# Embedding product and memory projection in five pieces at five places between the experts of a two-block kernel

## The chip, the cores and the metric

The kernel runs on one core of a Trainium2 chip. The time is that of one execution of the whole program on the device, in microseconds (us); a smaller one is better.

## The reference

Two transformer blocks follow each other on 256 tokens of width 1024, all in float32. The first has pooling and neighbourhood attention, an expert layer (16 experts, each takes its 32 best tokens), and an embedding that is mixed in behind it. The second has sparse, recurrent and memory attention and a feed-forward part. What the change touches, cut to its core:

```
# expert layer: each expert e takes its 32 tokens xe of h
a = xe @ w_gate[e]; b = xe @ w_up[e]          # 32x1024 @ 1024x2048
ye = (silu(a) * b) @ w_down[e]                # 32x2048 @ 2048x1024
x[tokens of e] += gate * ye                   # 16 experts

# embedding, first block: needs only p and w_ple_proj
e = rms_norm(p @ w_ple_proj, norm_ple_post)   # 256x256 @ 256x1024
x = x + sigmoid(rms_norm(x, norm_ple) @ w_ple_gate) * e

# memory keys and values, second block: need only mem and w_kv
kv = rmsnorm(mem, g_mem) @ w_mem_kv           # 256x1024 @ 1024x1024
k, v = kv[:, :512], kv[:, 512:]
```

The embedding product and the memory projection depend on nothing that the experts compute, so they may stand at any place between them.

## The kernel before, in words

**The ring.** Weights pass through a ring of six slots in SBUF of 2 MB each (`ring`, lines 205 and 206); three other buffers serve as slots 6, 7 and 8 for expert 0 only: `later`, `turned_T` and `gains`. Each slot has two semaphores, `full` (a load has landed) and `free` (it may be written again). `Ring.load` (line 161) waits for `free` of its slot and issues the load (line 169); `Ring.arrived` (line 176) is the other side. SyncE (SP) issues all weight loads, in one fixed order written out by hand; while it waits for one slot, no later load is issued, even where its slot lies free.

**An expert.** It has twelve loads of 2 MB: n = 0 to 3 for the gate, 4 to 7 for up, 8 to 11 for down. `around(rot)` gives the slots: load n goes into slot (n + rot) mod 6, so each slot serves twice. TensorE's `expert` (line 965) gathers the 32 tokens (32 matmuls) and the gate values (16 small ones), waits for `xe_sb`, which VectorE gives when it has scaled the gathered input (line 1514), multiplies slot by slot with 16 matmuls of 512 columns each, hands a slot back after its last matmul, transposes the hidden values (line 993), multiplies by the down weights, and adds the result to the tokens (8 matmuls, line 1011). ScalarE and VectorE evict in between (lines 621 to 630 and 1512 to 1527); VectorE adds to x (line 1526). The slot of the last load, n = 11, is handed back at the very end (line 1014).

**The order.** `PARTS = (1, 5, 5, 5)`: expert 0 is written out, and then come three loops over five experts, each a body of its own in the code of every engine. What lies between the loops is written out by hand on each engine:

- behind expert 5 (lines 1025 to 1052 of TensorE): four transposes of p (line 1029), the 16 transposes of the normed memory (`turn(1, mx, 0)`, line 839), the embedding product from slot 3 (16 matmuls of 512 columns), and the first half of the memory projection, the keys, from slot 4 (64 matmuls of 256 columns), evicted by ScalarE into `later` (line 656), whereupon slot 4 is handed back (line 1052);
- behind expert 10 (lines 1055 to 1061): the second half, the values, from slot 2 (32 matmuls of 512 columns), evicted at line 661.

ScalarE evicts the embedding product (line 647) and sums its squares (line 653). VectorE turns the memory into its transposed and scaled form (line 1397), waits for the squares (line 1539) and for the rows (line 1540), computes the inverse root (from line 1369) and scales the embedding (line 1543). The rows are four loads that ScalarE issues right behind expert 0 (lines 638 to 640) into `gains`, which is free only then; they are written to all 128 partitions.

**Slots at the two breaks.** The loop before the first break ends on slot 2; then come slot 3 (embedding, 1 MB), slot 4 (memory, 2 MB) and the loop that begins with slot 5. That loop ends on slot 4; then comes slot 2 (memory, 2 MB), and the last loop begins with slot 3. Slots 5, 0 and 1 are passed over there.

Of the kernel before, what the change touches and what calls it, by code (L numbers as in the profile page):

```python
# [46 lines left out]
PARTS = (1, 5, 5, 5)  # L47
# [77 lines left out]
FIRST_SLOTS = [0, 1, 2, 3, 6, 8, 4, 5, 7, 0, 1, 2]  # L125

# [68 lines left out]
def two_blocks(nc, a, out):  # L195
    ctx = ExitStack()
    with ctx:
# [215 lines left out]
        def _(sp):  # L413
# [3 lines left out]
            def whole(s, name, i):  # L417

                n = a[name].shape[2]
                return slot[s][:, 0:n], packed[name][bass.ds(i * P, P), :]  # L420
# [20 lines left out]
            def experts(part, rot):  # L441
                with sp.Fori(0, PARTS[part]) as i:
                    r.enter(i, {s: (2, 2) for s in range(SLOTS)})
                    expert(i + sum(PARTS[:part]), around(rot))
                    r.leave(PARTS[part])

            expert(0, FIRST_SLOTS)
            experts(1, 3)

            r.load(3, whole(3, "w_ple_proj", 0))  # L450
            r.load(4, whole(4, "w_mem_kv", 0))
            experts(2, 5)
            r.load(2, whole(2, "w_mem_kv", 1))
            experts(3, 3)
# [75 lines left out]
        def _(act):  # L530
# [110 lines left out]
            experts(1)  # L641

# [7 lines left out]
            for t in range(NT):  # L650
                if t:
                    act.wait_ge(e_sq, t)
                act.activation(junk, uP[:, t, :], ACT.Square, accum_out=sq[:, 24 + t:25 + t]).then_inc(e_sq, 1)
            for b in range(2):
                act.wait_ge(mkv_ps, b + 1)
                act.activation(kTm[:, b * 512:(b + 1) * 512], bank[b], ACT.Copy).then_inc(mkv_sb, 1)
            experts(2)

            for b in range(2):
                act.wait_ge(mkv_ps, b + 3)  # L660
                act.activation(vm[:, b, :], bank[2 + b], ACT.Copy).then_inc(mkv_sb, 1)
            experts(3)
# [164 lines left out]
        def _(pe):  # L827
            r = Ring(pe, full, free)

            def mm(o, l, rr, start=True, stop=True):  # L830
                return pe.matmul(o, l, rr, start=start, stop=stop)  # L831
# [191 lines left out]
            experts(1, 3)  # L1023

            pe.wait_ge(in_p, 16)
            pe.wait_ge(x_acc, 4 * sum(PARTS[:2]))
# [8 lines left out]
            for t in range(NT):  # L1035
                for h in range(2):
                    for k in range(2):
                        ins = mm(bank[4 + 2 * t + h], pT[:, k, t * P:(t + 1) * P], wple[:, k, h * 512:(h + 1) * 512], k == 0, k == 1)
                    ins.then_inc(e_ps, 1)
            pe.wait_ge(hT_done, 12)  # L1040
            r.arrived(4, 1)
            for h in range(4):
                for k in range(KC):
                    ins = mm(bank[h // 2][:, (h % 2) * T:(h % 2) * T + T], strip[4][:, k, h * P:(h + 1) * P],
                             hT[:, k, :], k == 0, k == KC - 1)
                    if h == 0 and k == 0:
                        ins.then_inc(free[3], 1)
                if h % 2:
                    ins.then_inc(mkv_ps, 1)
            pe.wait_ge(mkv_sb, 2)  # L1050
            pe.wait_ge(e_sb, 4)
            pe.sem_inc(free[4], 1)
            experts(2, 5)

            r.arrived(2, 1)
            for t in range(NT):
                for k in range(KC):
                    ins = mm(bank[2 + t], hT[:, k, t * P:(t + 1) * P], strip[2][:, k, :], k == 0, k == KC - 1)
                ins.then_inc(mkv_ps, 1)
            pe.wait_ge(mkv_sb, 4)  # L1060
            pe.sem_inc(free[2], 1)
            experts(3, 3)
# [299 lines left out]
        def _(dve):  # L1362
# [173 lines left out]
            experts(1)  # L1536
# [8 lines left out]
            experts(2)  # L1545
            experts(3)
# [293 lines left out]
def packed_strips(inputs):  # L1840
# [27 lines left out]
    out["w_mem_kv"] = strips(get("w_mem_kv_2"), 512)  # L1868
# [37 lines left out]
```

## Time and profile before

| | |
|---|---|
| median of three runs | 1838.83 us (1835.06 to 1841.44) |
| the profiled execution: its time | 1839.95 us |
| the profiled execution: its span | 1838.2 us |
| TensorE matmuls, busy | 1487.7 us, 81% of the span |
| VectorE, ScalarE, GpSimd busy | 20%, 10%, 1% |
| mean granted clock of TensorE | 0.893 |
| moved by DMA | 517.48 MB, 282 GB/s on average |

The span goes from the first instruction to the last of the profiled execution; its time is a little longer, since start and end lie around it. "PE" is TensorE's matmuls, "PEld" its weight loads, "DVE" VectorE, "ACT" ScalarE, "POOL" GpSimd, "SPq" the queue of SyncE. The granted clock is 1.00 for the full 2.4 GHz and 0.50 for 1.2 GHz. A line such as L831 is that of a helper through which all matmuls go.

### The profile page before, as it was taken

Reading aid. Unit: us, or ns where it says so; the run is one execution under the profiler, and the core shown is the slowest. Engines: PE = TensorE matmul, PEld = TensorE weight load, DVE = VectorE, ACT = ScalarE, POOL = GpSimd, SP = SyncE. Lnnn points to the kernel's source line nnn. Section 1 sums busy time; section 2 is a strip of 40 time slices with the busy share of each in tenths; the row PEclk is TensorE's granted clock in tenths of the full one; section 3 lists DMA queues with packets and bytes.
Section 4 is the critical chain, followed back from the end, with each engine's and each line's share of the span. In section 5 each row is a group of like instructions: output and inputs, shape, how many; then the busy total and the mean of one; then the engine's idle time right before and its main releaser. Section 6 shows DMA issues by size and latency. Waiting matters only on the chain.

```text
span 1838.2 us, 20016 instructions
## 1 busy us (share of the span) xinstructions
PE 1487.7 (81%) x7980; PEld 830.8 (45%) x7980; DVE 364.9 (20%) x1052; ACT 183.0 (10%) x503; POOL 14.7 (1%) x55
## 2 busy tenths in 40 slices
PE   6997676676686766687666668899999999999997
PEld 3444221122242212231222213887777888577774
DVE  3543101001110000000001003353354010410002
ACT  1220000000010000000000001132233000100000
POOL 0000000000000000000000000000000000000000
PEclk9997887888888868877888779899999999999999
DMA  9265999999989999999999994121140345123431
GB/s 352 95 261 211 425 429 429 428 429 428 427 351 428 428 429 429 429 388 428 428 429 429 429 429 190 59 107 48 60 194 26 114 169 226 62 114 152 181 147 46
DMA packets 46482, 517.48 MB, mean 282 GB/s; under 512 B 10736, under 2 KB 11632, under 8 KB 13936
## 3 DMA queue, kind: packets, MB, share of 16 engines
q1 hardware_dynamic: 37872, 509.62, 66.5%
q10 hardware_dynamic: 7952, 4.67, 1.0%
q0 software_dynamic: 624, 2.72, 0.4%
q8 instruction: 23, 0.38, 0.1%
q14 instruction: 11, 0.09, 0.0%
HBM read 515.43 MB, written 1.05 MB: 281 GB/s over the span
## 4 chain that ended last, share of the span: by engine, by line
PE 56%; DMA 37%; DVE 5%; issue 1%; ACT 1%; SPq 0%; PEldq 0%; ACTq 0%; DVEq 0%; POOL 0%
PE ps L831 54%; DMA ring<-in_experts 37%; PE ps L1149 1%; DVE scr L1522 1%; PE ps L839 1%; DVE turned_T L1397 1%; ACT xn L703 0%; DVE nt_ L1373 0%; DVE nt_ L1374 0%; DMA x<-in_x 0%; DVE scr L1769 0%; DVE nt_ L1375 0%; DVE x L1771 0%; DVE xn L1647 0%; ACT scr L709 0%
## 5 line engine op out<-in xcount | busy, mean ns | idle before, releaser
L831 PE MATMUL ps<-ring,scr 128*32 128x512 f32 (+1 forms) x3216 | 557.2, 758 | 237.6 <-DMA ring<-in_experts 231.2
L831 PEld LDWEIGHTS ps<-ring,scr 128*32 128x32 f32 (+1 forms) x3216 | 136.4, 132 | 617.5 <-DMA ring<-in_experts 358.8
L831 PE MATMUL ps<-turned_T,ring 128*128 128x256 f32 (+2 forms) x1984 | 385.4, 365 | 6.5 <-PE ps L831 2.3
L831 PEld LDWEIGHTS ps<-turned_T,ring 128*128 128x128 f32 (+1 forms) x1984 | 336.8, 187 | 55.1 <-issue 12.7
L831 PE MATMUL ps<-ring,turned_T 128*128 128x512 f32 (+3 forms) x544 | 176.6, 484 | 3.5 <-DVE turned_T L1397 2.5
L831 PE MATMUL ps<-scr 128*128 128x512 f32 (+10 forms) x624 | 158.5, 407 | 21.2 <-DVE scr L1522 13.0
L831 PEld LDWEIGHTS ps<-ring,turned_T 128*128 128x128 f32 x544 | 95.3, 196 | 80.3 <-issue 72.6
L831 PEld LDWEIGHTS ps<-scr 64*128 64x128 f32 (+3 forms) x624 | 86.7, 178 | 94.2 <-issue 41.2
L831 PE MATMUL ps<-scr,xn 128*128 128x32 f32 x512 | 68.1, 296 | 12.3 <-PE ps L831 8.4
L831 PEld LDWEIGHTS ps<-scr,xn 128*128 128x128 f32 x512 | 66.3, 213 | 24.3 <-issue 22.3
L1522 DVE COPY scr<-ps 128x512 f32<-128x512 f32 x16 | 11.1, 692 | 295.3 <-PE ps L831 295.3
L1519 DVE SCALAR_TENSOR_TENSOR scr<-scr,ps 128x512 f32<-128x512 f32 x16 | 11.0, 688 | 267.0 <-PE ps L831 267.0
L1526 DVE TENSOR_TENSOR x<-x,ps 128x512 f32<-128x512 f32 x64 | 44.0, 687 | 33.5 <-PE ps L831 33.5
L1783 DVE SCALAR_TENSOR_TENSOR scr<-scr,ps 128x256 f32<-128x256 f32 x22 | 9.3, 422 | 191.4 <-ACT scr L814 191.4
L1517 DVE SCALAR_TENSOR_TENSOR scr<-scr,ps 128x512 f32<-128x512 f32 x16 | 11.0, 688 | 162.2 <-ACT scr L625 162.2
L627 ACT ACTIVATE scr<-ps 128x512 f32<-128x512 f32 x16 | 9.6, 597 | 303.3 <-PE ps L993 303.3
L629 ACT ACTIVATE scr<-ps 128x512 f32<-128x512 f32 x16 | 9.6, 597 | 272.0 <-PE ps L831 272.0
L1751 DVE SCALAR_TENSOR_TENSOR scr<-scr,ps 128x512 f32<-128x512 f32 x8 | 5.5, 687 | 126.6 <-PE ps L831 126.6
L703 ACT ACTIVATE xn<-ps,scr 128x128 f32<-128x128 f32 x64 | 26.0, 420 | 31.0 <-DVE scr L1636 31.0
L814 ACT ACTIVATE scr<-ps 128x256 f32<-128x256 f32 x22 | 8.4, 384 | 206.6 <-PE ps L831 206.6
L831 PE MATMUL ps<-later,ring 128*128 128x256 f32 x128 | 28.9, 379 | 0.0
L831 PE MATMUL ps<-ring,xn 128*128 128x512 f32 x64 | 27.7, 594 | 0.5 <-PE ps L831 0.5
(237 smaller groups left out, 668.4 us busy)
## 6 DMA issues: line engine op xcount, KB each, us to landing
ring<-in_experts SPq DMA_DIRECT2D x189, 2048.0 KB, 24.6
ring<-in_w_ffn_in SPq DMA_DIRECT2D x11, 2048.0 KB, 8.8
ring<-in_w_merge SPq DMA_DIRECT2D x8, 1536.0 KB, 6.3
ring<-in_w_ffn_down SPq DMA_DIRECT2D x11, 1024.0 KB, 4.8
ring<-in_w_in SPq DMA_DIRECT2D x4, 2048.0 KB, 19.5
ring<-in_w_out SPq DMA_DIRECT2D x4, 2048.0 KB, 13.7
ring<-in_w_ml SPq DMA_DIRECT2D x4, 2048.0 KB, 7.8
ring<-in_w_nsa SPq DMA_DIRECT2D x4, 2048.0 KB, 7.7
```

The source lines that it names most:

```text
L627: act.activation(hTe.rearrange("p c n -> p (c n)"), bank[2], ACT.Copy).then_inc(ht_sb, 1)
L629: act.activation(ysb[:, 0:512], bank[4], ACT.Copy).then_inc(y_sb, 1)
L703: e = act.activation(Pn[:, o, b, c], bank[2 * o + b][:, c], ACT.Exp, bias=nmN[:, o, b, t:t + 1], accum_out=smN[:, o, b, t:t + 1])
L831: return pe.matmul(o, l, rr, start=start, stop=stop)
L839: ins = pe.transpose(bank[b0 + 2 * t + h][:, k * P:(k + 1) * P], src[:, t, kk * P:(kk + 1) * P], ident)
L1149: ins = pe.transpose(bank[4 + b][:, c * P:(c + 1) * P], Pn[:, i % 2, b, c * P:(c + 1) * P], ident)
L1397: dve.tensor_tensor(hT[:, 4 * h:4 * h + 4, t * P:(t + 1) * P], bank[b0 + 2 * t + h].rearrange("p (k t) -> p k t", k=4), gain, ALU.mult)\
L1517: chain(dve.scalar_tensor_tensor(out=thE, in0=thE, scalar=1.0, in1=bank[0], op0=ALU.add, op1=ALU.mult))
L1519: dve.scalar_tensor_tensor(out=hE, in0=thE, scalar=0.5, in1=bank[1], op0=ALU.mult, op1=ALU.mult)\
L1522: dve.tensor_copy(ysb[:, 512:1024], bank[5]).then_inc(y_sb, 1)
L1526: dve.tensor_tensor(x[:, t, h * 512:(h + 1) * 512], x[:, t, h * 512:(h + 1) * 512], bank[(6, 4)[t] + h], ALU.add).then_inc(x_acc, 1)
L1783: chain(dve.scalar_tensor_tensor(out=vF[:, par, f, :], in0=thF[:, par, f, :], scalar=1.0, in1=b[:, 0:T], op0=ALU.add, op1=ALU.mult))
```

## The change

`PARTS` becomes `(1, 3, 3, 3, 3, 3)`. The embedding product stands behind expert 0. The memory projection is cut into four pieces of 256 columns of the weights each (1 MB), behind experts 3, 6, 9 and 12; the piece behind experts 3, 6, 9 and 12 takes slot 4, 5, 0 and 1. The loops begin with slots 4, 5, 0, 1 and 3. Keys (pieces 0 and 1) and values (pieces 2 and 3) are each evicted from one bank of 512 columns. On VectorE the turn of the memory, the waits for squares and rows, and the scaling of the embedding stand between experts 0 and 1.

```
-PARTS = (1, 5, 5, 5)
+PARTS = (1, 3, 3, 3, 3, 3)
+ROTS = [4, 5, 0, 1]
...
SyncE
             expert(0, FIRST_SLOTS)
-            experts(1, 3)
-
             r.load(3, whole(3, "w_ple_proj", 0))
-            r.load(4, whole(4, "w_mem_kv", 0))
-            experts(2, 5)
-            r.load(2, whole(2, "w_mem_kv", 1))
-            experts(3, 3)
+            for n in range(4):
+                experts(1 + n, ROTS[n])
+                r.load(ROTS[n], whole(ROTS[n], "w_mem_kv", n))
+            experts(5, 3)
...
ScalarE
-            experts(1)
-
             act.wait_ge(pT_ps, 1)
...
                 act.activation(junk, uP[:, t, :], ACT.Square, accum_out=sq[:, 24 + t:25 + t]).then_inc(e_sq, 1)
+            experts(1)
             for b in range(2):
                 act.wait_ge(mkv_ps, b + 1)
                 act.activation(kTm[:, b * 512:(b + 1) * 512], bank[b], ACT.Copy).then_inc(mkv_sb, 1)
-            experts(2)
-
+                experts(2 + b)
             for b in range(2):
                 act.wait_ge(mkv_ps, b + 3)
-                act.activation(vm[:, b, :], bank[2 + b], ACT.Copy).then_inc(mkv_sb, 1)
-            experts(3)
+                act.activation(vm[:, :, b * 256:b * 256 + 256], bank[b].rearrange("p (t n) -> p t n", t=NT), ACT.Copy)\
+                   .then_inc(mkv_sb, 1)
+                experts(4 + b)
...
TensorE
             expert(0, FIRST_SLOTS)
-            experts(1, 3)
-
             pe.wait_ge(in_p, 16)
-            pe.wait_ge(x_acc, 4 * sum(PARTS[:2]))
+            pe.wait_ge(x_acc, 4)
...
+            pe.wait_ge(e_sb, 4)
+            pe.sem_inc(free[3], 1)
             pe.wait_ge(hT_done, 12)
-            r.arrived(4, 1)
-            for h in range(4):
-                for k in range(KC):
-                    ins = mm(bank[h // 2][:, (h % 2) * T:(h % 2) * T + T], strip[4][:, k, h * P:(h + 1) * P],
-                             hT[:, k, :], k == 0, k == KC - 1)
-                    if h == 0 and k == 0:
-                        ins.then_inc(free[3], 1)
-                if h % 2:
-                    ins.then_inc(mkv_ps, 1)
-            pe.wait_ge(mkv_sb, 2)
-            pe.wait_ge(e_sb, 4)
-            pe.sem_inc(free[4], 1)
-            experts(2, 5)
-
-            r.arrived(2, 1)
-            for t in range(NT):
-                for k in range(KC):
-                    ins = mm(bank[2 + t], hT[:, k, t * P:(t + 1) * P], strip[2][:, k, :], k == 0, k == KC - 1)
+            experts(1, ROTS[0])
+
+            for n in range(4):
+                s, b = ROTS[n], n % 2
+                r.arrived(s, 1)
+                w = slot[s][:, 0:KC * 256].rearrange("p (k n) -> p k n", k=KC)
+                for h in range(2):
+                    for k in range(KC):
+                        if n < 2:
+                            ins = mm(bank[b][:, h * T:h * T + T], w[:, k, h * P:(h + 1) * P], hT[:, k, :], k == 0, k == KC - 1)
+                        else:
+                            ins = mm(bank[b][:, h * T:h * T + T], hT[:, k, h * P:(h + 1) * P], w[:, k, :], k == 0, k == KC - 1)
                 ins.then_inc(mkv_ps, 1)
-            pe.wait_ge(mkv_sb, 4)
-            pe.sem_inc(free[2], 1)
-            experts(3, 3)
+                pe.wait_ge(mkv_sb, n + 1)
+                pe.sem_inc(free[s], 1)
+                experts(2 + n, (ROTS + [3])[n + 1])
...
VectorE
             expert(0)
-            experts(1)
             gained(1, 0)
 
             dve.wait_ge(e_sq, 2)
...
-            experts(2)
-            experts(3)
+            for n in range(1, 6):
+                experts(n)
...
-    out["w_mem_kv"] = strips(get("w_mem_kv_2"), 512)
+    out["w_mem_kv"] = strips(get("w_mem_kv_2"), 256)
```

## Rows read from the trace of the kernel before

**Rows 1.** The page: rate of transfers in 40 slices, the chain, the costliest group

```profile
GB/s 352 95 261 211 425 429 429 428 429 428 427 351 428 428 429 429 429 388 428 428 429 429 429 429 190 59 107 48 60 194 26 114 169 226 62 114 152 181 147 46
...
PE 56%; DMA 37%; DVE 5%; issue 1%; ACT 1%; SPq 0%; PEldq 0%; ACTq 0%; DVEq 0%; POOL 0%
...
L831 PE MATMUL ps<-ring,scr 128*32 128x512 f32 (+1 forms) x3216 | 557.2, 758 | 237.6 <-DMA ring<-in_experts 231.2
```

**Rows 2.** The chain in order of time: start, us, what; copies of experts 4, 15

```profile
433.00 0.70 DVE scr L1522
...
1103.37 0.70 DVE scr L1522
```

**Rows 3.** Windows: length, busy (instructions) of PE to POOL, PEclk, DMA share, GB/s

```profile
571.40:630.10 58.70, 39.60 (x252) 13.93 (x252) 5.26 (x9) 2.17 (x4) 0.29 (x1) 0.83 1.01 429
...
516.00:540.00 24.00, 22.80 (x182) 11.68 (x180) 1.11 (x2) 1.58 (x3) 0.29 (x1) 0.93 0.72 281
...
804.00:814.00 10.00, 9.58 (x21) 3.88 (x20) 2.75 (x4) 0.00 (x0) 0.00 (x0) 0.91 0.65 238
```

**Rows 4.** The timeline of the first break: start, us, what [idle before <-releaser]

```profile
483.66 1.93 PE L831 MATMUL ps<-ring,scr 128*32 128x512 f32 x16 [1.59 <-DMA ring<-in_experts]
...
488.56 3.53 PE L831 MATMUL ps<-ring,scr 128*32 128x512 f32 x16 [2.97 <-DMA ring<-in_experts]
...
496.65 0.69 DVE L1526 TENSOR_TENSOR x<-x,ps 128x512 f32<-128x512 f32 x1 [0.17 <-PE ps L831]
...
506.57 13.98 PE L831 MATMUL ps<-turned_T,ring 128*128 128x256 f32 x64
...
506.77 0.60 ACT L647 ACTIVATE scr<-ps 128x512 f32<-128x512 f32 x1 [1.12 <-PE ps L831]
...
509.76 0.17 DVE L1369 TENSOR_SCALAR nt_<-sq 128x2 f32<-128x2 f32 x1 [8.68 <-ACT scr L653]
...
512.13 2.61 DVE L1543 SCALAR_TENSOR_TENSOR scr<-scr,rst,gains 128x1024 f32<-128x1024 f32 x2
...
521.56 3.75 PE L831 MATMUL ps<-scr,xn 128*128 128x32 f32 x32 [1.01 <-ACT later L656]
...
525.35 0.42 DVE L1514 TENSOR_TENSOR scr<-ps,vecs 128x256 f32<-128x256 f32 x1 [10.61 <-PE ps L831]
...
525.91 13.92 PE L831 MATMUL ps<-ring,scr 128*32 128x512 f32 x112
```

**Rows 5.** Line 169 in short windows: one issue and its time to landing

```profile
L169 SPq DMA_DIRECT2D ring<-in_experts x1: 333/333/333, 521.5 to 521.5; - x1
...
DMA to landing us min/median/max: 7.7/7.7/7.7
...
L169 SPq DMA_DIRECT2D ring<-in_w_ple_proj x1: 338/338/338, 467.4 to 467.4; - x1
...
DMA to landing us min/median/max: 23.6/23.6/23.6
```

**Rows 6.** The timeline of the second break, SyncE's queue

```profile
808.17 35.98 SPq L169 DMA_DIRECT2D ring<-in_experts  x12
```

**Rows 7.** Behind expert 0: the last row load and a weight load, to landing

```profile
L640 ACTq DMA_DIRECT2D gains<-in_ml_head_g x1: 462/462/462, 198.6 to 198.6; - x1
...
DMA to landing us min/median/max: 28.2/28.2/28.2
...
L169 SPq DMA_DIRECT2D ring<-in_experts x1: 333/333/333, 205.7 to 205.7; - x1
...
DMA to landing us min/median/max: 23.4/23.4/23.4
```

**Rows 8.** The timeline behind expert 0: last sum, first matmuls of expert 1

```profile
197.22 0.69 DVE L1526 TENSOR_TENSOR x<-x,ps 128x512 f32<-128x512 f32 x1 [0.17 <-PE ps L831]
...
202.01 6.88 PE L831 MATMUL ps<-ring,scr 128*32 128x512 f32 x48
```

## Prediction

> **What bounds the kernel now.** I read the page first: the transfer rate in 40 slices, the chain that ended last, the costliest groups. From slice 5 to slice 24 (about 184 to 1103 us) the rate stands at 425 to 429 GB/s, with two dips, 351 in slice 12 and 388 in slice 18. The chain names the transfers of expert weights for 37% of the span. The largest group of TensorE, the expert products, sat idle for 231.2 us until a weight load had landed [rows 1]. So the expert phase is paced by one stream of 2 MB loads. At 429 GB/s [rows 3] a load takes 2.097/0.429 = 4.89 us and an expert with its 12 loads 58.7 us. TensorE worked for 39.6 of the 58.7 us of such a stretch [rows 3]. Work that is put between experts is therefore free as long as the stream does not stop. The stream stops in one way only: SP has no free slot into which it may issue. Six slots make about five loads in the queue.
>
> Next the chain in order of time. The last expert product copy of expert 4 starts at 433.00 and that of expert 15 at 1103.37 [rows 2], 670.4 us for 11 experts. Eleven experts are 132 x 4.89 = 645.5 us, and the 5 MB of embedding and memory weights 12.2 us, together 657.7. About 12.7 us were lost. The windows show where: from 516 to 540 us the transfers are busy 0.72 of the time, from 804 to 814 us 0.65, against 1.01 in a full stretch [rows 3]. That is 24 x 0.29/1.01 = 6.9 us and 10 x 0.36/1.01 = 3.6 us, 10.5 us in sum.
>
> The timeline says why. In the first break TensorE takes its last expert matmul at 488.56 and the first one of the next expert at 525.91 [rows 4]. Between them lie the embedding product and 64 memory matmuls of 13.98 us, and an eviction after which slot 4 is handed back. The load into it is issued at 521.5 and lands 7.7 us later, although a load behind another takes 4.9 [rows 5]: the queue was empty, and an empty queue costs 7.7 - 4.9 = 2.8 us more until the data flow. The second break has 14 us of TensorE work as well, but the cause there is the order of slots: SP waits at slots 2, 3 and 4, the last freed by the end of the expert, and only at 808.17 does it issue on [rows 6], while slots 5, 0 and 1 lay free.
>
> **The change part by part.** *The two breaks of before go.* With a 1 MB piece there are 32 matmuls of 256 columns, half of 13.98 = 7.0 us, then 1.0 us for the eviction (520.55 to 521.56, [rows 4]). I follow a break at full clock, counted from the landing of the expert's last load: 8.1 us until TensorE has done with it (488.56 to 496.65), 7.0 and 1.0 for the piece, 4.35 for the gather of the next expert (521.56 to 525.91), about 3.8 until its first slot is free (3.7 by 202.01 to 205.73, [rows 7, 8]). That is 24.3 us. In the queue at the landing stand the piece (2.45 us) and six expert loads (29.35), and a new issue must come 2.8 us before they end: 29.0 us. 4.7 us are to spare, and the stream goes on. In the break before the last three experts slot 2 is passed over: the tight issue is then that into slot 1, freed 8.1 + 7.0 + 1.0 = 16.1 us after the landing, and needed by 2.45 + 4 x 4.89 - 2.8 = 19.2 us. 3.1 us to spare. Gain: 10.5 us, between 10.5 and 12.7, the whole loss. Against this the clock: TensorE is granted 0.83 on average in such a stretch [rows 3], so the reserve can be used up now and then. Over four breaks I take +0.5 us; the bounds are 0 and 6 (1.5 at each break, a third of a piece and of the sums before it at half clock beyond what is to spare).
>
> *The embedding product moves from behind expert 5 to behind expert 0.* Here the order on VectorE matters more than the work. Behind the product VectorE waits for the squares of ScalarE and for the four row loads (norm rows and head gain), and only then does it scale the embedding, and only behind that does it make the gathered input of expert 1, for which TensorE waits before its first expert matmul. Before the change that wait came 300 us after the rows had been issued. Now it comes at once. ScalarE issues the rows when expert 0 is done; the last is issued at 198.6 and lands 28.2 us later, at 226.8 [rows 7], because it shares with the saturated stream. Everything else is ready earlier: the last sum of expert 0 ends at 197.22 + 0.69 = 197.9; from that point (497.34 in the old break) it was 10.0 us until the last eviction had ended (507.37) and 12.4 until VectorE began the scale (509.76) [rows 4], so 207.9 and 210.3. VectorE then goes on at 226.8 instead of 210.3. The scale takes 4.98 us (509.76 to 514.74), the gathered input and the start of TensorE 0.56 (525.35 to 525.91) [rows 4]: the first matmul of expert 1 comes at 226.8 + 5.0 + 0.6 = 232.3, where before it was at 202.01 [rows 8]. Its slot is free 3.8 us later, at 236.1, and the load into it lands 7.7 us after, at 243.8.
>
> What does the stream have until then? The load issued at 205.7 lands 23.4 us later, at 229.1 [rows 7]. It is the seventh counted from the first load into slot 3. After the change the first of these seven is the embedding weight of 1 MB, so the seventh lands 2.45 us earlier, at 226.7; its slot is handed back at 207.9, in time. The eighth would land at 231.6 if the stream went on, and lands at 243.8: loss 12.2 us. The bounds: nothing, if the rows come in time (rival B); 12.2 with the first slot's 16 matmuls in the 3.7 us of [rows 7, 8], and 1.6 less, 10.6, if they go as fast as those at 483.66 (1.93 us against 3.53 at 488.56, [rows 4]). That the 12.2 us are taken is shown by the nearest case in the trace, the stall of [rows 5], where each us of late issue was a us of late landing.
>
> *More code.* The expert body stands in six places instead of four. Each new body is fetched, and its fetch goes by the same engines. Of the 12.7 us lost before, 2.2 are not in the two gaps; two new bodies stand in that stretch, so at most 1.1 us each. After the change there are two more: between 0 and 2.2, and I take the middle, +1.2 us, since nothing says how the 2.2 are shared out.
>
> *Four loads of 1 MB instead of two of 2 MB.* The embedding weights are such a load: issued at 467.4, landed 23.6 us later at 491.0 [rows 5], 2.4 us behind the load that TensorE took at 488.56 [rows 4]. A load in a full queue costs its bytes and nothing else: 0. The Trainium skill speaks against this change here: "DMA: Bandwidth & Descriptors", section "Anatomy of one DMA", gives every transfer a fixed cost of about 2.0 us besides its bytes. By it two more loads would cost an estimated 4 us. The row above does not agree for a transfer that stands behind others.
>
> *Evictions and products otherwise:* the same number of columns, the value half as 32 matmuls of 256 instead of 16 of 512 twice, four evictions of 512 columns as before: 0, under the waits for data.
>
> **The sum.** -10.5 (gaps) + 12.2 (wait for the rows) + 0.5 (clock) + 1.2 (code) = +3.4 us. The profiled execution took 1839.95 us for a span of 1838.2, so 1843.3 on its scale. It lay 1.1 us above the median of the three runs, 1838.83; on the median's scale it is 1842.2.
>
> **The rivals.** A measurement of this kernel can tell about 0.3% from no change, 5.5 us: under 1833.3 is faster, over 1844.3 slower.
>
> A, the forecast, 0.70: the gain of two breaks is given back in one stall on the row loads between 212 and 232 us. 1842.2. Its own range by the bounds of the terms: from -12.7 + 10.6 = -2.1 to -10.5 + 12.2 + 6 + 2.2 = +9.9, so 1837 to 1849. For it: the order of VectorE's work in the code and the landing at 226.8.
>
> B, 0.15: the rows come early enough, or VectorE passes their wait sooner than I reckon. Then the first matmul of expert 1 is at 210.3 + 5.0 + 0.6 = 215.9, the slot free at 219.7, needed by 226.7 - 2.8 = 223.9. No loss: 3.4 - 12.2 = -8.8 us, 1830.0. Against it: the rows ran beside a full stream before, and that is the same until 226.7.
>
> C, 0.10, the other side: the memory pieces drain the ring at every break, because TensorE is granted half its clock there. It decides from 4.7 us of extra time on. A piece at half clock takes 7.0 us more and the sums before it 1.7 more: 8.7 - 4.7 = 4.0 us lost, four times 16 us, on top of A: 1858. For it: a mean of 0.83 says that a third of such a stretch ran at half clock [rows 3]. Against it: in the first break the memory matmuls took 0.218 us each for 256 columns, which is the full clock [rows 4].
>
> D, 0.05: each load pays the 2.8 us of an empty queue. Two more loads, +5.6 us on A: 1848. Against it stands the embedding load [rows 5]. The fixed cost that the Trainium skill gives in "DMA: Bandwidth & Descriptors", section "Anatomy of one DMA", is this rival's rule.
>
> **How the numbers follow.** A reaches above 1844.3 in about a quarter of its cases (slow clock in several breaks, code at its bound), 0.16, and lies within 0.3% in the rest. B is faster. C and D are slower. Faster 0.15, same 0.54, slower 0.31. The range goes from 1831, which takes in half of B, to 1851, which takes in A and D and leaves out C.
>
> **What the profile of the changed kernel would show.** TensorE idle from about 212 to 232 us, released by VectorE; VectorE's first step of the inverse root at about 226.8; the transfers idle from about 227 to 239 us; the load after it landing 7.7 us after its issue. The rate at 425 to 429 GB/s from there to the end of the phase, with no window under 0.9 at the four breaks; last expert copy about 3 us later than 1103.37. I would be wrong if the transfers run on through 227 to 239 us (then B), or if the windows behind experts 3, 6, 9 and 12 show gaps of over 1 us each (then C).

## The result and the profile after

The changed kernel took 1847.29 us (median of 13 runs, 1841.7 to 1850.78), the kernel before 1836.88 beside it (13 runs, 1834.95 to 1841.44): the ratio is 1.0051, 95% interval 1.0039 to 1.0062, so 9 us slower. The ratios in this document lie close to the ratio of the means of all runs; the medians, given beside them, can differ from them by a us or two, here 10.4 us instead of 9. The profiled execution took 1847.29 us as well, with a span of 1845.5. On the page of the changed kernel, the lines that answer to [rows 1]:

```profile
GB/s 350 95 261 211 371 357 428 428 427 428 429 428 427 428 428 429 427 428 428 428 427 429 428 428 171 58 106 48 60 193 26 114 164 227 64 114 146 184 148 46
...
PE 54%; DMA 38%; DVE 5%; issue 2%; ACT 1%; SPq 0%; ACTq 0%; PEldq 0%; DVEq 0%; POOL 0%
PE ps L831 52%; DMA ring<-in_experts 35%; DMA gains<-in_ml_head_g 2%; DMA ring<-in_rpb 1%; PE ps L1143 1%; DVE scr L1516 1%; DVE turned_T L1391 1%; PE ps L839 0%; ACT xn L703 0%; DVE nt_ L1367 0%; DVE nt_ L1368 0%; DMA x<-in_x 0%; DVE scr L1762 0%; ACT scr L709 0%; DVE nt_ L1369 0%
```

The dips in slices 12 and 18 are gone. In their place slices 5 and 6 fell to 371 and 357 GB/s, and the chain has a member that it did not have before: the transfer of the head gain, 2% of the span. The timeline of the changed kernel behind expert 0, which answers to [rows 8] and the second half of [rows 4]:

```profile
199.02 0.45 ACTq L641 DMA_DIRECT2D gains<-in_ml_head_g  x1
...
207.79 0.60 ACT L646 ACTIVATE scr<-ps 128x512 f32<-128x512 f32 x1 [1.12 <-PE ps L831]
...
212.48 1.08 PE L831 MATMUL ps<-consts,scr 128*32 128x128 f32 x16
...
227.24 0.17 DVE L1363 TENSOR_SCALAR nt_<-sq 128x2 f32<-128x2 f32 x1 [25.14 <-DMA gains<-in_ml_head_g]
...
229.62 2.61 DVE L1536 SCALAR_TENSOR_TENSOR scr<-scr,rst,gains 128x1024 f32<-128x1024 f32 x2
232.44 0.42 DVE L1508 TENSOR_TENSOR scr<-ps,vecs 128x256 f32<-128x256 f32 x1 [0.21 <-DVE scr L1536]
233.00 13.38 PE L831 MATMUL ps<-ring,scr 128*32 128x512 f32 x108 [19.43 <-DVE scr L1508]
```

VectorE stands for 25.14 us. The squares were there at 210.8, the last row only at 227.1. Then it scales the embedding, and only then makes the gathered input, for which TensorE had stood 19.43 us. The windows of the changed kernel (columns as in [rows 3]) show the stream in that time and at the four breaks:

```profile
197.60:226.90 29.30, 14.08 (x85) 9.35 (x84) 3.17 (x5) 5.67 (x10) 0.29 (x1) 0.75 0.94 392
226.90:239.40 12.50, 6.40 (x48) 1.74 (x52) 4.96 (x15) 0.00 (x0) 0.00 (x0) 0.63 0.15 31
...
390.00:420.00 30.00, 26.00 (x172) 14.27 (x176) 4.26 (x7) 1.88 (x4) 0.29 (x1) 0.94 1.01 427
568.00:600.00 32.00, 29.77 (x188) 15.85 (x184) 4.56 (x7) 2.17 (x4) 0.29 (x1) 0.85 1.01 428
748.00:780.00 32.00, 27.92 (x188) 14.83 (x184) 4.56 (x7) 2.17 (x4) 0.29 (x1) 0.94 1.01 429
925.00:960.00 35.00, 29.20 (x192) 14.74 (x184) 4.55 (x7) 2.17 (x4) 0.29 (x1) 0.90 1.01 429
262.00:1104.00 842.00, 583.26 (x3676) 201.56 (x3672) 73.39 (x112) 32.83 (x60) 3.82 (x13) 0.83 1.01 428
```

From 226.9 to 239.4 us the transfers were busy 0.15 of the time. Then the load that ends the gap, issued at 236.8 (line 172 is the issuing line here):

```profile
L172 SPq DMA_DIRECT2D ring<-in_experts x1: 333/333/333, 236.8 to 236.8; - x1
...
DMA to landing us min/median/max: 7.6/7.6/7.6
```

It landed at 244.4. The one before it landed at 227.0, so 17.4 us lie between two loads where 4.9 is usual: 12.5 us lost. From 262 us on the stream ran at 428 GB/s for 842 us, over all four memory pieces, and none of the windows at the four breaks is under 1.01. The last expert load landed at 1104.0 instead of 1101.3.

That is +2.7 us, and the span is 7.3 us longer. The other 4.6 us came behind the last expert load: from its landing to the end it took 736.8 us before and 741.4 after, although the change touches nothing there. The experiments have this part as a question of its own.

### The profile page after: what moved, and what is told of

Same layout as the page of the kernel before. It is cut to its first block, busy times and chain, and to the rows that moved or that the text cites. A ratio compares the mean times of both kernels' runs of the same rounds, so it can differ in the third digit from the quotient of the medians.

```text
span 1845.5 us, 20067 instructions
## 1 busy us (share of the span) xinstructions
PE 1482.4 (80%) x8012; PEld 834.5 (45%) x8012; DVE 365.0 (20%) x1052; ACT 183.0 (10%) x503; POOL 14.7 (1%) x55
## 4 chain that ended last, share of the span: by engine, by line
PE 54%; DMA 38%; DVE 5%; issue 2%; ACT 1%; SPq 0%; ACTq 0%; PEldq 0%; DVEq 0%; POOL 0%
PE ps L831 52%; DMA ring<-in_experts 35%; DMA gains<-in_ml_head_g 2%; DMA ring<-in_rpb 1%; PE ps L1143 1%; DVE scr L1516 1%; DVE turned_T L1391 1%; PE ps L839 0%; ACT xn L703 0%; DVE nt_ L1367 0%; DVE nt_ L1368 0%; DMA x<-in_x 0%; DVE scr L1762 0%; ACT scr L709 0%; DVE nt_ L1369 0%
## 5 line engine op out<-in xcount | busy, mean ns | idle before, releaser
L831 PE MATMUL ps<-ring,scr 128*32 128x512 f32 (+1 forms) x3216 | 547.7, 746 | 246.9 <-DMA ring<-in_experts 222.4
L831 PE MATMUL ps<-ring,turned_T 128*128 128x256 f32 (+3 forms) x576 | 177.2, 467 | 3.9 <-DVE turned_T L1391 2.5
L831 PE MATMUL ps<-scr 128*128 128x512 f32 (+10 forms) x624 | 162.7, 414 | 21.6 <-DVE scr L1516 13.0
L831 PEld LDWEIGHTS ps<-ring,turned_T 128*128 128x128 f32 x576 | 101.3, 195 | 76.3 <-issue 67.1
```

## The experiments

Twelve runs were made, of eight new kernels and four repeats, in three lots, each lot on one chip and with its own times of the kernel before. Two theories stood at the start. Theory 1: the stream stops because VectorE stands at the row loads. Theory 2: the embedding work behind expert 0, or the five breaks, cost by themselves.

### The scaling of the embedding three experts later

```
             expert(0)
             gained(1, 0)
-            dve.wait_ge(e_sq, 2)
-            dve.wait_ge(in_rows, 16 * 4)
-            rsqrt(...)
-            ...
-            for n in range(1, 6):
+            experts(1)
+            dve.wait_ge(e_sq, 2)
+            dve.wait_ge(in_rows, 16 * 4)
+            rsqrt(...)
+            ...
+            for n in range(2, 6):
                 experts(n)
```

> The changed kernel with VectorE's waits for the squares and the rows, the inverse root and the scaling of the embedding moved from behind expert 0 to behind expert 3; TensorE, ScalarE and SyncE are as in the changed kernel. Theory 1 (the stream stops because VectorE stands at the row loads): the gap from 227 to 239 us goes, the load into slot 4 is issued at about 220 us, the time falls by the 12.5 us that the gap holds in the changed kernel's trace, from 1847.3 to about 1835. Theory 2 (the embedding work behind expert 0 costs by itself, or the five breaks do): the gap is only shortened and the time stays within 3 us of 1847.

Measured: 1833.48 us (6 runs), before 1838.46; ratio 0.9970 (0.9957 to 0.9983). The same windows in this kernel:

```profile
197.60:226.90 29.30, 24.26 (x168) 12.17 (x172) 3.86 (x7) 6.27 (x11) 0.30 (x1) 0.92 1.02 426
226.90:239.40 12.50, 9.99 (x48) 1.58 (x40) 0.00 (x0) 0.00 (x0) 0.00 (x0) 0.51 0.99 422
```

The gap is gone, 0.99 instead of 0.15, and with it the loss: from 1.0051 to 0.9970 of the kernel before are 15 us, 12.5 expected. Counted in the traces from the issue of the first row to the landing of the last expert load, the stream took 13.5 us less than in the three profiles of the changed kernel. Everything else of the change, the embedding product behind expert 0 and the four pieces, was left in. Theory 2 falls as the cause of the loss.

### Waiting for the one row that is needed

```
-    act.dma_start(grows[:, c, :], ...).then_inc(in_rows, 16)
+    act.dma_start(grows[:, c, :], ...).then_inc(in_rows if c else bias_sb, 16)
...
-            dve.wait_ge(in_rows, 16 * 4)
+            dve.wait_ge(bias_sb, 17)
...
             for n in range(1, 6):
                 experts(n)
+            dve.wait_ge(in_rows, 16 * 3)
```

GpSimd's later wait for the rows is cut from four to three as well.

> The changed kernel with VectorE waiting at the same place for the one row load that the scaling needs, the first of the four, and for the other three behind the last expert. In the changed kernel's trace the first row landed at 208.6 us and the last at 227.1. Theory 1: the scaling begins when the squares are there, at about 211, the first matmul of expert 1 comes at about 216 and the stream does not stop: 12.5 us less, about 1835, the same as with the late scaling. If the loss came from something else in VectorE's order at this place (the turn of the memory, the scaling of 2.6 us), it stays near 1847.

Measured: 1836.4 us (10 runs, 1828.26 to 1837.7), before 1838.46; ratio 0.9983 (0.9971 to 0.9995). The timeline of VectorE in this kernel:

```profile
210.84 0.17 DVE L1363 TENSOR_SCALAR nt_<-sq 128x2 f32<-128x2 f32 x1 [8.69 <-ACT scr L652]
...
216.04 0.42 DVE L1508 TENSOR_TENSOR scr<-ps,vecs 128x256 f32<-128x256 f32 x1 [0.21 <-DVE scr L1536]
```

The scaling stands at the place where the change put it; VectorE begins with the inverse root at 210.84, when the squares are there. The gathered input of expert 1 comes at 216.04 instead of 232.44, and the stream does not stop:

```profile
226.90:239.40 12.50, 7.08 (x44) 1.44 (x48) 0.00 (x0) 0.00 (x0) 0.00 (x0) 0.75 1.01 427
```

So neither the place nor the 5 us of scaling count, only the wait for all four rows. This is rival B's course of events, made by hand, 12 us faster than the changed kernel.

### The wait alone, in the kernel before

```
             expert(0)
+            dve.wait_ge(in_rows, 16 * 4)
             experts(1)
```

> The kernel before with one wait added on VectorE and nothing else: behind expert 0, ahead of the gathered input of expert 1, it waits for the four row loads. Theory 1: they land at about 227, the first expert matmul of expert 1 comes at 227.4 instead of 202.0, its slot is free at 231.2, the load into it lands at 238.9 instead of 234.0: 4.9 us longer. In the changed kernel the inverse root and the scaling (5.0 us) and the embedding load of 1 MB instead of 2 MB (2.45 us) come on top, which would make up its 12.5 us. If waiting at this place is hidden by the six slots: no change.

Measured: 1846.74 us (10 runs), before 1840.29; ratio 1.0038 (1.0026 to 1.0051), 7 us. One wait, and no work moved, costs nearly as much as the whole change, which loses more at this place (12.5 us in the stream) and gains some of it back at the breaks. Its timeline:

```profile
197.44 3.75 PE L831 MATMUL ps<-scr,xn 128*128 128x32 f32 x32 [0.39 <-PE ps L831]
...
224.27 0.42 DVE L1514 TENSOR_TENSOR scr<-ps,vecs 128x256 f32<-128x256 f32 x1 [26.49 <-DMA gains<-in_ml_head_g]
224.83 14.21 PE L831 MATMUL ps<-ring,scr 128*32 128x512 f32 x112 [23.01 <-DVE scr L1514]
```

The expectation of 4.9 us had an error in it: it counted the load into expert 1's first slot as the eighth behind expert 0, but without the embedding weights ahead of it it is the seventh, and was due at 228.8. It landed at 236.4, 7.6 us late. And the last row was there at 224.1, not at 227: it took 25.6 us from its issue instead of 28.2, at a place where the last queued weight load landed at 223.9 and the next was issued only at 228.7. That fits a row load that is late because it shares with the stream. How long it takes without any stream no run shows.

### The embedding product moved alone

The kernel before with its three loops of five and its two memory halves; only the embedding product, with VectorE's waits and scaling, stands behind expert 0, as in the change (slots: 3 for the embedding, then the first loop from slot 4).

```
             expert(0, FIRST_SLOTS)
-            experts(1, 3)
-
             r.load(3, whole(3, "w_ple_proj", 0))
+            experts(1, 4)
             r.load(4, whole(4, "w_mem_kv", 0))
             experts(2, 5)
```

> The kernel before with the embedding product alone moved behind expert 0; the memory projection stays in two halves of 2 MB behind experts 5 and 10, three loops of five. Theory 1: +12.4 us for the gap at 227 us, -7.4 us for the gap of the first break (14 + 1 us of memory work give 31.3 us until the first slot is free, against 31.4 that the queue holds), the second gap of 3.3 stays: +5 us on the kernel before, 1842. If the part of the measured difference that the forecast lacked (about 6 us) comes with the early embedding, 1848; if it comes with the pieces and the two more loop bodies, 1842.

Measured: 1846.94 us (5 runs), before 1838.46; ratio 1.0044 (1.0030 to 1.0058), 8 us instead of the 5 of the forecast. Its windows at 227 us, at the first and at the second break:

```profile
226.90:239.40 12.50, 6.73 (x48) 1.79 (x52) 4.95 (x15) 0.00 (x0) 0.00 (x0) 0.64 0.15 38
525.00:548.00 23.00, 21.56 (x177) 10.98 (x175) 1.11 (x2) 1.58 (x3) 0.29 (x1) 0.93 0.93 384
810.00:825.00 15.00, 14.15 (x33) 6.16 (x34) 3.12 (x5) 0.87 (x2) 0.00 (x0) 1.00 0.87 347
```

The gap at 227 us is the same as in the changed kernel. At the first break 23 x 0.08/1.01 = 1.8 us are still lost, at the second 15 x 0.14/1.01 = 2.1 us. So a break with 14 us of memory work has about nothing to spare, as worked out, and the loss at the first break falls from 6.9 to 1.8 us once the embedding product is out of it. From the landing of the last expert load to the end this kernel took 737.7 us, as the kernel before, so its 8 us are in the stream: 1107.4 for the last landing is 6.1 us over the first profile of the kernel before and 9.7 over the second, which is shown below.

### The same with the scaling behind expert 5

```
-            for n in range(1, 4):
+            experts(1)
+            dve.wait_ge(e_sq, 2)
+            dve.wait_ge(in_rows, 16 * 4)
+            ...
+            for n in range(2, 4):
                 experts(n)
```

> The kernel before with the embedding product alone moved behind expert 0, as in the run of that kind, but VectorE's waits and the scaling behind expert 5 instead of behind expert 0. Theory 1: the gap of 12.5 us at 227 us goes, the last expert load lands at 1107.4 - 12.5 = 1094.9 instead of 1107.4, the time is 1834 or 5 us under the kernel before: the embedding product behind expert 0 costs nothing by itself and relieves the first break. If the early product costs by itself, the time stays over that of the kernel before.

Measured: 1832.35 us (10 runs), before 1837.23; ratio 0.9970 (0.9957 to 0.9982). The gap at 227 us is gone (busy 0.99), and the last expert load landed at 1088.5, earlier than the 1094.9 expected: expert 0 had ended 1.4 us earlier than in the run with the embedding alone, and the two breaks lost nearly nothing here (transfers busy 1.01 from 500 to 540 us and 0.97 from 790 to 815). Moving the embedding product up is a gain of 5 us once VectorE does not wait there. The ratio is the same as that of the late scaling with four pieces: the four pieces at four breaks bring nothing that can be measured on top.

### Each piece computed twice

```
-                for h in range(2):
+                for h in (0, 1, 0, 1):
```

Each memory piece is multiplied twice into the same bank, the second product overwriting the first.

> The changed kernel with each memory piece computed twice into the same bank (64 matmuls of 256 columns, 14 us, in place of 32 and 7). Theory 1 with 4.7 us to spare at three breaks and 3.1 at the last one: the stream loses 7.0 - 4.7 = 2.3 us three times and 3.9 once, about 11 us, 1858. If the pieces already use up the reserve: four times 7, 1875. If the reserve is over 7 us: no change, 1847.

Measured: 1858.08 us (4 runs), before 1838.46; ratio 1.0106 (1.0090 to 1.0123), against 1.0051 of the changed kernel: 10 us for 28 us of added matmuls. The windows of this kernel at the four breaks:

```profile
415.00:426.00 11.00, 11.00 (x100) 3.08 (x96) 0.69 (x1) 0.60 (x1) 0.00 (x0) 0.92 0.87 346
593.00:615.00 22.00, 18.03 (x160) 8.22 (x160) 1.11 (x2) 1.44 (x3) 0.30 (x1) 0.91 0.82 320
780.00:792.00 12.00, 12.00 (x108) 3.25 (x100) 0.69 (x1) 0.60 (x1) 0.00 (x0) 0.92 0.91 365
954.00:966.00 12.00, 10.99 (x96) 6.29 (x98) 0.42 (x1) 0.98 (x2) 0.30 (x1) 0.86 0.80 309
```

Lost against a share of 1.01: 1.5, 4.1, 1.2 and 2.5 us, 9.3 in sum, where three times 2.3 and once 3.9 were forecast, 10.8. The landings give more: from the issue of the first row to the last expert load the stream took 13.1 us longer than on average in the changed kernel. The reserve at a break, worked out from the two sums, is thus 4 to 5 us, near the 4.7 of the forecast; single breaks differ from it by some us, and why was not measured. Rival C needs it to be used up by a piece of 7 us, which no profile of the changed kernel shows: from slice 7 to slice 24 the rate is never under 426 GB/s in the three.

### The unchanged kernels again

> The changed kernel once more, unchanged, on this chip. The profile shows another execution: the stream up to the last expert load should again lose about 12.5 us at 227 us and nothing at the four breaks. Theory 3 (what the forecast lacked lies behind the last expert load, in stretches at half clock): from the landing of the last expert load to the end it took 741.4 us against 736.8 in the kernel before; here it may take anything between 737 and 745, and the total moves with it. If instead the breaks lose time in some executions, the landings show it.

> The kernel before once more, unchanged, for a second profile. By theory 3 the landing of the last expert load comes again at 1101 us, within 1 us, and the part behind it varies with TensorE's clock by some us, against 736.8 in the first profile.

> The changed kernel a third time, for one more profile. Theory 3: the last expert load lands at 1101 to 1104 us as in the two others, and the part behind it takes 741 to 746 us, longer than the 737 of the kernel before. If this part is pure chance from execution to execution, it is as likely to take 737.

Measured: the changed kernel 1847.21 us (7 runs) against 1840.29, ratio 1.0039 (1.0024 to 1.0053), and 1845.01 in the third lot; the kernel before 1837.0 in its second profiled execution. What the profiles give, in us from the start of the span, with the other kernels beside them:

| kernel | expert 0 done, first row issued | last expert load landed | from there to the end | span |
|---|---|---|---|---|
| before, first profile | 197.2 | 1101.3 | 736.8 | 1838.2 |
| before, second | 197.6 | 1097.7 | 737.5 | 1835.2 |
| changed, first | 197.7 | 1104.0 | 741.4 | 1845.5 |
| changed, second | 195.8 | 1101.5 | 746.4 | 1847.9 |
| changed, third | 195.7 | 1101.8 | 741.4 | 1843.2 |
| wait alone | 197.1 | 1107.8 | 737.1 | 1844.9 |
| embedding alone | 197.4 | 1107.4 | 737.7 | 1845.0 |
| the same, scaling late | 196.0 | 1088.5 | 738.9 | 1827.4 |
| piece twice | 197.2 | 1116.3 | 738.9 | 1855.2 |
| scaling late | 197.2 | 1089.8 | 745.0 | 1834.8 |
| first row | 197.7 | 1090.6 | 744.9 | 1835.5 |
| rows alone, in the kernel before | 197.1 | 1097.3 | 736.8 | 1834.1 |
| scaling and rows late, first | 197.8 | 1086.9 | 738.2 | 1825.1 |
| scaling and rows late, second | 195.4 | 1084.4 | 738.2 | 1822.6 |

The three executions of the changed kernel are on average 2.9 us later at the last load (1102.4 against 1099.5) and 5.9 us longer behind it (743.1 against 737.2), which together are the 8.8 us between the mean spans. The second and third of them had expert 0 done about 2 us earlier than the first, ahead of all that was changed. Counted from there the stream took 904.1 and 900.1 us in the kernel before and 906.4, 905.7 and 906.1 in the changed one, 3.9 us more on average. So the greater part of the measured difference, 5.9 us, lies where the change has changed nothing. The windows from the last landing on about 88 us, and then the 61 behind them, of the kernel before (second profile), the changed kernel (first) and again the changed kernel (second); the third number from the end is PEclk:

```profile
1097.70:1185.70 88.00, 74.39 (x582) 50.65 (x583) 35.04 (x119) 13.95 (x31) 0.69 (x5) 0.88 0.34 140
1185.70:1246.70 61.00, 59.06 (x311) 47.33 (x310) 25.82 (x87) 18.12 (x61) 1.30 (x8) 0.98 0.23 81
```

```profile
1104.00:1196.00 92.00, 78.38 (x582) 51.73 (x583) 35.04 (x119) 13.96 (x31) 0.70 (x5) 0.83 0.32 130
...
1196.00:1257.40 61.40, 59.27 (x312) 47.47 (x311) 25.84 (x87) 18.12 (x61) 1.59 (x9) 0.98 0.22 80
```

```profile
1101.50:1195.50 94.00, 80.58 (x582) 55.00 (x583) 35.05 (x119) 13.96 (x31) 0.68 (x5) 0.81 0.31 127
1195.50:1258.00 62.50, 60.37 (x306) 47.72 (x305) 25.82 (x87) 18.14 (x61) 1.40 (x9) 0.94 0.22 78
```

The same 582 matmuls take 88, 92 and 94 us, with VectorE and ScalarE at the same busy time, and the granted clock is 0.88, 0.83 and 0.81. The clock is enough to account for it: 0.05 less over 92 us is 4.6 us of work at full clock. The second execution of the changed kernel has one more low stretch behind that.

The place can be told more closely. In the kernel before (first profile):

```profile
1101.38 1.93 PE L831 MATMUL ps<-ring,scr 128*32 128x512 f32 x16 [1.54 <-DMA ring<-in_experts]
1104.11 3.70 PE L831 MATMUL ps<-scr 128*128 128x512 f32 x8 [0.81 <-DVE scr L1522]
...
1101.30:1112.00 10.70, 5.63 (x24) 1.86 (x24) 5.55 (x19) 3.16 (x9) 0.00 (x0) 1.00 1.01 432
```

In the changed kernel (first profile):

```profile
1104.08 3.64 PE L831 MATMUL ps<-ring,scr 128*32 128x512 f32 x16 [1.82 <-DMA ring<-in_experts]
1108.54 6.13 PE L831 MATMUL ps<-scr 128*128 128x512 f32 x8 [0.81 <-DVE scr L1516]
...
1104.00:1116.00 12.00, 9.78 (x24) 2.97 (x24) 3.45 (x5) 1.66 (x4) 0.00 (x0) 0.61 1.00 418
```

These are the last 24 matmuls of expert 15, behind the last load, where nothing hides them. At full clock they took 1.93 and 3.70 us; in the changed kernel most of them ran at half clock. From the last landing to the first transposition behind the experts it was 11.5 us in both profiles of the kernel before and 15.7, 14.4 and 15.7 us in the three of the changed kernel. In the first and third that is 4.2 of the 4.6 us. Just ahead of it half clock costs nothing: 16 matmuls of 3.36 us at 1096.47 in the kernel before stand between idle times of 2.5 and 1.5 us in which TensorE waits for loads. Behind the last load there is no such wait. What makes the chip grant the lower clock just there is not settled. It is not the five loops as such, since the kernel with doubled pieces has them and took 738.9 us, and that with late rows 738.2; and mere chance from execution to execution does not look likely, though so few profiles cannot exclude it: the changed kernel took over 741 us three times and the kernels with three loops 738.9 or less six times, and the first and third profile of the changed kernel and the one with the first row show the same 3.64 and 6.1 us here. The last three rows of the table belong to the next section. Theory 3 is shown as to the place and the clock, and open as to the cause.

The second profile of the kernel before shows one thing more. Its last expert load landed 3.6 us before that of the first. The window of its second break, which answers to the last of [rows 3]:

```profile
798.00:812.00 14.00, 12.43 (x40) 5.01 (x41) 3.44 (x5) 0.60 (x1) 0.00 (x0) 1.00 1.00 398
```

No gap here. TensorE ran at full clock through the end of the expert (its last 8 matmuls took 3.70 us, 5.38 in the first profile) and handed back slot 4 before the queue had run dry. The gap of the second break, which the forecast booked as a gain of 3.6 us, is there in some executions only: by the landings 3.3 us in the first profile, none in the second, 3.2 us with the wait alone and with the rows alone.

### Three rows later

```
-            for c, n in enumerate(("norm_ple_post", "g_post_mix_2", "g_post_ffn_2")):
-                act.dma_start(grows[:, c, :], ...).then_inc(in_rows, 16)
-            act.dma_start(hgrow, ...).then_inc(in_rows, 16)
+            act.dma_start(grows[:, 0, :], a["norm_ple_post"]...).then_inc(in_rows, 16)
...
                 experts(4 + b)
+            for c, n in enumerate(("g_post_mix_2", "g_post_ffn_2")):
+                act.dma_start(grows[:, 1 + c, :], ...).then_inc(in_rows, 16)
+            act.dma_start(hgrow, ...).then_inc(in_rows, 16)
...
-            dve.wait_ge(in_rows, 16 * 4)
+            dve.wait_ge(in_rows, 16)
...
+            dve.wait_ge(in_rows, 16 * 4)
             post(0, 0.5)
```

The late scaling, and the three rows that only the second block needs are loaded behind the last expert.

> The kernel with the late scaling, and in addition three of the four row loads (1.25 MB written to all partitions: two norm rows and the head gain, which only the second block needs) are issued by ScalarE behind the last expert, where the transfers have idle time, instead of behind expert 0. The rows took 4.5 us from the stream between 197 and 227 us; three of four leave it, 2.5 of 4.5 by bytes being 1.31 of 1.84 MB, so 3.2 us less than with the late scaling: about 1830.5, if the gain is not lost behind the experts. A rival: the clock of TensorE decides behind the experts, and the gain vanishes in its spread: no difference from the late scaling.

> The fastest kernel so far once more on this chip: 14 us under the kernel before, with a spread of 2 us. The profile shows whether the part behind the last expert load again takes 738 us, as in its first profile, or 745 as with the late scaling alone.

Measured: 1826.02 us (6 runs) against 1840.29, ratio 0.9923 (0.9910 to 0.9936), and in the next lot 1828.2 us (8 runs, 1824.32 to 1832.43) against 1837.23, ratio 0.9947 (0.9929 to 0.9964). It beats both kernels. Its window behind expert 0 has the stream full, at 427 GB/s and a share of 1.01:

```profile
197.60:226.90 29.30, 25.90 (x181) 12.58 (x180) 4.29 (x8) 6.27 (x11) 0.29 (x1) 0.94 1.01 427
```

The last expert load landed at 1086.9 and 1084.4, 2.9 and 5.4 us earlier than with the late scaling (in the second, expert 0 had ended 1.8 us earlier too); 1.31 MB at 429 GB/s are 3.1 us. Behind it the two executions took 738.2 us each, where the late scaling took 745.0. The rest of the gain is there. From the issue of the first row to the last landing the stream took 3.4 us less than with the late scaling in both, 3.2 expected. The second lot did not repeat the narrow spread of the first.

The rows alone, with the same edit in the kernel before (VectorE's wait at the scaling is for one row, and the one for all four stands behind, as above):

> The kernel before with one thing changed: three of the four row loads are issued by ScalarE behind the last expert instead of behind expert 0. Their 1.31 MB leave the stream: the last expert load lands 3 us earlier than the 1101.3 and 1097.7 of the two profiles of the kernel before, and the time is 3 us shorter, about 1836 where the kernel before has 1839, if the part behind the experts stays at 737 us. If the row loads were hidden in idle time anyway: no difference.

Measured: 1835.38 us (12 runs) against 1837.23, ratio 0.9979 (0.9967 to 0.9991), 4 us by the ratio and 2 by the medians, 3 expected. The last expert load landed at 1097.3, 4.0 us earlier than in the first profile of the kernel before, which has the gap at the second break as this kernel has, and 0.4 earlier than in the second, which has not. The part behind took 736.8 us. In the kernel before four expert loads beside the rows landed 5.7 to 6.2 us apart; with three rows gone one did (5.9), and the next ones landed 4.9 apart. The rows were not hidden; they cost the stream their bytes.

## Why the prediction was right, and where it was off

The measured 1847.3 lies in the range of 1831 to 1851, and the direction was that of the sum. The forecast of 1842.2 was 5 us too low, and the case that it held likeliest, within 0.3%, did not come: the kernel is slower by 0.5%, to which it had given 0.31. Against the kernel before the forecast was +3.4 us; measured are 9 by the ratio and 10.4 by the medians. What was right was the mechanism of the stream; the rest came from a part that the prediction did not look at, and that the time still fell into the range was owed to its width.

- *The wait for the rows, +12.2 us.* Right step by step. VectorE went on at 227.2 (226.8 forecast), the first matmul of expert 1 came at 233.0 (232.3), the issue at 236.8 (236.1), the landing 7.6 us later (7.7), the loss was 12.5 us (12.2). The late scaling, the first row and the wait alone show that this wait is the cause.
- *The two gaps of before, -10.5 us.* They went, in every profile of the changed kernel. As a gain it was counted too high: in the second profile of the kernel before the second gap is not there. The profile that was read had a gap that hangs on the clock at the end of expert 10, and its own time lay 3 us above the median of 13 runs.
- *The reserve at a break, 4.7 us, and +0.5 us for the clock.* Right in the main: no gap at the four breaks, and 9.3 us (by the windows) or 13.1 us (by the landings) lost with doubled pieces, 10.8 by the same sum. The upper bound of 6 us for the clock does not follow from its own words: a third of 7.0 and 1.7 us more is 2.9 us at a break, less than the 4.7 to spare, so nothing would be lost.
- *More code, +1.2 us.* Not measured by itself. The sum of stream terms was +3.4 us; measured from the issue of the first row to the last landing was +2.3 between the first profiles and +3.9 between the means. Of the +2.3, 12.5 less 10.7 for the two gaps by their landings are 1.8, so about 0.5 us are left for code and clock together, where 1.7 were forecast; against the second profile, which has the first gap alone, it is 0.9.
- *Four loads of 1 MB, 0.* The stream ran at 428 GB/s over all of them. The load into an empty queue took 7.6 us against 4.9; a load that stands in a queue cost its bytes and nothing else. The Trainium skill ("DMA: Bandwidth & Descriptors", section "Anatomy of one DMA") gives about 2.0 us of fixed cost for each DMA, fitted to those that GpSimd issues; SyncE issues these. Here 2.7 us came once, with the empty queue, and none for loads in a queue.
- *What was missing.* The step that failed is the silent assumption that what comes behind the expert phase takes as long as before. It took 5.9 us longer on average, at a lower granted clock, in the first profile nearly all of it in the last 24 matmuls of expert 15, at half clock in place of full. The forecast had put the clock into the breaks alone, with 0 to 6 us, and there it cost less than 1 us. Why the clock is lower behind the last load in the changed kernel stays open.

Of the rivals, B and the forecast differ by whether VectorE's wait holds; it holds, and the two kernels that take it away land at 1833 and 1836. C and D did not occur.

## What to carry to other kernels

When work is moved to another place in the order, look at each engine for the waits that move with it, and ask when what they wait for was issued: a wait that had 300 us of cover had none when its other condition, the squares, was met 12 us behind the issue, and it stood on VectorE, ahead of a step that TensorE and so the weight stream needed. Make a wait as narrow as its use, one row and not four, and load late what is used late when the stream is the bound. Compare a gain of a few us with a second profile of the kernel before: one of the two gaps was there only in one of them.

## What the runs showed of the hardware

- Row loads that are written to all partitions slow a full weight stream beside them: its loads landed up to 6.2 us apart instead of 4.9. Of 1.84 MB in four such loads the last landed 28.1 us after its issue. In the run with the wait alone, where the last queued weight load landed at 223.9, it took 2.6 us less. With 1.31 MB of them out of the stream the kernel before was 4 us faster by the ratio, 2 by the medians.
- A load of 2 MB into an empty queue landed 7.6 to 7.7 us after its issue; loads behind one another landed 4.9 us apart (2 MB) and 2.4 us apart (1 MB).
- The part behind the experts took from 736.8 us in the kernel before to 746.4 in the changed one, with the same matmuls and the same busy time of VectorE and ScalarE in the windows compared, at a granted clock of 0.90 and 0.81 over the first 88 to 94 us. A gain in one phase may be given back there: against the first profile of the kernel before the late scaling had its last load 11.5 us earlier and a span only 3.4 us shorter.
